# Third block of a three-block network: copies, logarithms, banks and the first C·B products placed elsewhere between the normalisation and the state-space stage

## The reference, cut to what matters

```
x = first_block(...)                                   # ends with rms_norm(h, final_norm_g)
h = _rmsnorm(x, norm_w) * (1 + scale) + shift          # "C" in the kernel; x's own norm is "D"
proj = einsum("bsd,de->bse", h, w_in)                  # 1024 x 1024 by 1024 x IN_COLS
z_ssm, xbc, dt_raw, q, k, v, z_att, f_logit, g_logit = split(proj)
xbc = silu(causal_depthwise_conv(xbc, conv_w, conv_b)) # 4 taps; 1280 channels = 10 blocks of 128
xs, B, C = split(xbc, [1024, 1152])                    # B, C: 2 groups x 64 states
dt = softplus(dt_raw + dt_bias); a = -dt * exp(a_log)  # the step sizes
cb = einsum("bclgn,bcsgn->bgcls", C, B)                # per chunk of 128 tokens: "C.B"
y = (cb * L) @ (xs * dt) + (terms of earlier chunks) + d_skip * xs
```

## Time and profile before

| | us |
|---|---|
| median of 3 runs (lowest, highest) | 2923.1 (2921.4, 2924.74) |
| the profiled execution | 2922.75 |
| its span | 2921.4 |
| PE busy | 2786.5, 95% |
| DVE busy | 1591.5, 54% |
| ACT busy | 1356.0, 46% |
| POOL busy | 851.7, 29% |

### The profile page before, as it was taken

The page is one execution under the profiler, slowest core; times in us unless marked ns, Lnnn a source line. Parts: engine busy times, 40 slices in busy tenths (PEclk is TensorE's granted clock), DMA queues, the critical chain, the costliest instruction groups (busy, mean ns, idle before and its releaser), DMA issues.

```text
span 2921.4 us, 36300 instructions
## 1 busy us (share of the span) xinstructions
PE 2786.5 (95%) x13800; PEld 2278.1 (78%) x13800; DVE 1591.5 (54%) x2766; ACT 1356.0 (46%) x2486; POOL 851.7 (29%) x668
## 2 busy tenths in 40 slices
PE   8999999999999999998997999999999999999997
PEld 6778777777788888887774877778787888887875
DVE  6667774644388888887467765531002444433034
ACT  5657864334367666674435334541113333333122
POOL 0334441223345445542121222133221111112331
PEclk9999999999999999999998999999999999999998
DMA  3101131211100000003110200133111000101231
GB/s 130 40 29 41 40 130 64 94 66 37 33 10 10 10 10 10 17 23 139 49 58 27 101 29 23 30 98 90 58 51 37 30 30 30 30 30 44 72 116 72
DMA packets 54443, 148.77 MB, mean 51 GB/s; under 512 B 6144, under 2 KB 14976, under 8 KB 54272
## 3 DMA queue, kind: packets, MB, share of 16 engines
q1 hardware_dynamic: 54272, 146.46, 15.3%
HBM read 129.66 MB, written 16.78 MB: 50 GB/s over the span
## 4 chain that ended last, share of the span: by engine, by line
PE 85%; DVE 6%; ACT 5%; issue 3%; POOL 1%; DMA 0%; ACTq 0%; DVEq 0%; POOLq 0%
PE ps L327 79%; PE ps L445 4%; ACT t L311 1%; PE ps L2611 1%; PE ps L768 1%; DVE t L1665 0%; ACT t L807 0%; DVE t L898 0%; DVE t L2957 0%; DVE t L867 0%; POOL t L318 0%; DVE t L1295 0%; DVE t L1678 0%; ACT L394 0%; POOL t L2862 0%
## 5 line engine op out<-in xcount | busy, mean ns | idle before, releaser
L327 PE MATMUL ps<-t,t 128*128 128x512 f32 (+5 forms) x11912 | 2622.8, 379 | 107.8 <-ACT t L2056 9.5
L327 PEld LDWEIGHTS ps<-t,t 128*128 128x128 f32 (+2 forms) x11912 | 2075.9, 185 | 583.3 <-issue 113.9
L318 POOL TENSOR_TENSOR t<-t,t 128x1024 fp32r<-128x1024 f32 (+2 forms) x169 | 359.9, 2130 | 1267.6 <-ACT t L311 1267.0
L311 ACT ACTIVATE t<-t 128x1024 fp32r<-128x1024 f32 (+2 forms) x205 | 187.0, 913 | 678.6 <-PE ps L327 678.6
L1721 POOL TENSOR_SCALAR t<-t,t 128x1024 f32<-128x1024 f32 x128 | 145.2, 1134 | 183.0 <-DVE t L1671 180.0
L1665 DVE TENSOR_TENSOR t<-ps,t 128x512 fp32r<-128x512 f32 x256 | 164.2, 682 | 15.8 <-ACT t L1582 13.9
L445 PE MATMUL ps<-t,t 128*128 128x128 f32 x1176 | 160.5, 274 | 12.7 <-DVE t L1665 7.6
L445 PEld LDWEIGHTS ps<-t,t 128*128 128x128 f32 x1176 | 131.9, 141 | 36.5 <-issue 24.7
L1678 DVE TENSOR_REDUCE t<-ps 128x1 f32<-128x1024 f32 x128 | 154.1, 1204 | 2.2 <-PE ps L327 2.2
L1582 ACT ACTIVATE t<-ps 128x512 fp32r<-128x512 f32 x256 | 140.2, 592 | 11.3 <-PE ps L445 7.2
L1590 ACT ACTIVATE t<-ps,t 128x1024 f32<-128x1024 f32 x128 | 142.8, 1116 | 1.9 <-DVE t L1678 1.5
(11 more groups left out here) (219 smaller groups left out, 2429.6 us busy)
## 6 DMA issues: line engine op xcount, KB each, us to landing
t<-in_wflat SPq DMA_DIRECT2D x156, 512.0 KB, 3.6
t<-in_wada SPq DMA_DIRECT2D x48, 256.0 KB, 3.9
t<-in_xT SPq DMA_DIRECT2D x16, 512.0 KB, 7.0
t<-in_wflat SPq DMA_DIRECT2D x32, 128.0 KB, 2.0
hd<-t SPq DMA_DIRECT2D x8, 512.0 KB, 3.0
t<-hd SPq DMA_DIRECT2D x8, 512.0 KB, 7.5
x2d<-t SPq DMA_DIRECT2D x8, 512.0 KB, 6.8
md<-t SPq DMA_DIRECT2D x16, 256.0 KB, 4.4
```

Of the source, the lines that this page charges most:

```text
L311: ac.activation(parts(i)[0][:, 0:n], raw[i % 2][:, 0:n], ACT.Copy).then_inc(*on.up(ac, "whi", i))
L318: e.tensor_tensor(lo[:, 0:n], raw[i % 2][:, 0:n], hi[:, 0:n], ALU.subtract) \
L327: return pe.matmul(o, l, r, start=start, stop=stop)
```

## The change

Four edits in these stages:

1. The first two copies out of PSUM (`conv_in` of blocks 0 and 1, half 0) stand in ACT's program after the fourth high part of the second half, where they stood after `rstd`.
2. The two logarithms of `rstd` "D" stand together, and then the two exponentials. `w_hi` of `DTF` and of block 2 follow at once.
3. The two halves of `DTF` go to banks 4 and 5 (last used by the totals of norm "C"), and don't take a turn of `next_bank`; every later bank of the stage moves.
4. `products(0)` stands on PE between the two halves of block 7, the last of the convolution, in two banks that `next_bank` gives; `products_out(0)` stands on DVE before the taps of block 7's second half.

```
-            def scalar():
+            def scalar(first_inputs):
...
                 for k in range(8):
                     high_part(k, 1)
+                    if k == 3:
+                        first_inputs()
+                for hf in range(2):
+                    on.wait_ge(ac, "sums/tot", "D", hf)
+                    ac.activation(RB[:, half(hf)], ps[:, bank["D", hf], :], ACT.Ln, bias=eps[:, 0:1], scale=1.0 / T).then_inc(*on.up(ac, "ln", "D", hf))
+                for hf in range(2):
+                    on.wait_ge(ac, "ln", "D", hf)
+                    ac.activation(RB[:, half(hf)], RB[:, half(hf)], ACT.Exp, scale=-0.5).then_inc(*on.up(ac, "rstd", "D", hf))
...
-                            bank[DTF, x] = lin(DTF, x, next_bank(*every), Uh, Ul, need_c, [("dt", x)])
+                            bank[DTF, x] = lin(DTF, x, 4 + x, Uh, Ul, need_c, [("dt", x)])
...
+                    if (n, hf) == (7, 1):
+                        products(0, (next_bank(*every), next_bank(*every)))
                     bank[XB[q], hf] = lin(XB[q], hf, next_bank(*every), Uh, Ul, need_c, [("conv in", q, hf)])
...
                     if (n, hf) == (4, 0):
                         sums()
+                    if (n, hf) == (7, 1):
+                        products_out(0)
...
-                norm_scalar()
-                for hf in range(2):
-                    rstd("D", hf, bank["D", hf], RB, T)
+                def first_inputs():
+                    for x in range(2):
+                        conv_in(*todo[x])
+
+                norm_scalar(first_inputs)
+                w_hi(XB[0] + 2)
+                w_hi(XB[1] + 2)
...
-                    if x == 1:
-                        w_hi(XB[0] + 2)
-                        w_hi(XB[1] + 2)
+                    if x > 1:
+                        conv_in(q, n, hf)
                     if x:
                         smooth(*todo[x - 1])
...
-                products(0)
                 for g in range(2):
                     segments(8 * g)
...
-                            products(1)
+                            products(1, (4, 5))
...
             def vector():
                 everything_in(dv)
-                products_out(0)
```

More of the change, by code:

```diff
@@ L1896, in program, with products, products_out @@
         tv = tot[:, :].rearrange("p (c h) -> p c h", c=8)
+        def products(g, banks):
+            rg = slice(64 * g, 64 * g + 64)
+            for c2, b in enumerate(banks):
+                bank["cb", g, c2] = b
+                wait_bank(b)
+                on.wait_ge(pe, "xb", 9, 1)
+                for c in range(4):
+                    cc = slice((4 * c2 + c) * P, (4 * c2 + c + 1) * P)
+                    t = mm(ps[:, b, c * P:(c + 1) * P], BT[rg, cc], CT[rg, cc], True, True)
+                t.then_inc(*on.up(pe, "cb", g, c2))
+                freed[b] = [("cb out", g, c2)]
+        def products_out(g):
+            for c2 in range(2):
+                on.wait_ge(dv, "cb", g, c2)
+                src = ps[:, bank["cb", g, c2], :].rearrange("p (c n) -> p c n", c=4)
+                dv.tensor_tensor(CB[:, 4 * c2:4 * c2 + 4, :], src, tri.unsqueeze(1).to_broadcast([P, 4, P]), ALU.mult) \
+                    .then_inc(*on.up(dv, "cb out", g, c2))
         def stage_conv():
@@ L2051, in scalar @@
                         w_hi(XB[q] + 2)
-                    on.wait_ge(ac, "mm", XB[q], hf)
-                    earlier = [p for p in range(q) if X_ORDER[p] % 2 == n % 2]
-                    if earlier:
-                        on.wait_ge(ac, "conv", earlier[-1], 1, 3)
-                    ac.activation(xin[n % 2][:, 3 + hf * H:3 + hf * H + H], ps[:, bank[XB[q], hf], :], ACT.Copy).then_inc(*on.up(ac, "conv in", q, hf))
-                    if x == 1:
-                        w_hi(XB[0] + 2)
-                        w_hi(XB[1] + 2)
+                    if x > 1:
+                        conv_in(q, n, hf)
                     if x:
@@ L2062, in scalar, with conv_in @@
                 smooth(*todo[-1])
+            def conv_in(q, n, hf):
+                on.wait_ge(ac, "mm", XB[q], hf)
+                earlier = [p for p in range(q) if X_ORDER[p] % 2 == n % 2]
+                if earlier:
+                    on.wait_ge(ac, "conv", earlier[-1], 1, 3)
+                ac.activation(xin[n % 2][:, 3 + hf * H:3 + hf * H + H], ps[:, bank[XB[q], hf], :], ACT.Copy).then_inc(*on.up(ac, "conv in", q, hf))
             def smooth(q, n, hf):
@@ L2169, in tensor @@
                         if t == 2:
-                            products(1)
+                            products(1, (4, 5))
                 on.ends(pe, "end ssd", "pe")
-            def products(g):
-                rg = slice(64 * g, 64 * g + 64)
-                for c2 in range(2):
-                    b = 4 + c2
-                    wait_bank(b)
-                    on.wait_ge(pe, "xb", 9, 1)
-                    for c in range(4):
-                        cc = slice((4 * c2 + c) * P, (4 * c2 + c + 1) * P)
-                        t = mm(ps[:, b, c * P:(c + 1) * P], BT[rg, cc], CT[rg, cc], True, True)
-                    t.then_inc(*on.up(pe, "cb", g, c2))
-                    freed[b] = [("cb out", g, c2)]
             def gate_pe(t, hf):
@@ L2284, in vector @@
                 on.ends(dv, "end ssd", "dv")
-            def products_out(g):
-                for c2 in range(2):
-                    on.wait_ge(dv, "cb", g, c2)
-                    src = ps[:, 4 + c2, :].rearrange("p (c n) -> p c n", c=4)
-                    dv.tensor_tensor(CB[:, 4 * c2:4 * c2 + 4, :], src, tri.unsqueeze(1).to_broadcast([P, 4, P]), ALU.mult) \
-                        .then_inc(*on.up(dv, "cb out", g, c2))
             def pair_pick(t):
```

## The result

| | before | changed |
|---|---|---|
| median (lowest, highest), us | 2922.74 (2921.4, 2924.74), 4 runs | 2905.82 (2903.6, 2908.13), 4 runs |
| profiled execution, us | 2922.75 | 2905.76 |
| its span, us | 2921.4 | 2904.4 |

The ratio is 0.9941, interval 0.9928 to 0.9954. The direction was right and the size wrong: the larger part of what is missing in the forecast lies behind the edited stages.

The account below looks back on a forecast made before the run. PE was taken to bound the kernel, ending the chain for 85% of the span. Gains 8.2 + 1.55 + 1.6 = 11.35 from 2922.75 gave 2911.4, forecast 2911.5 us, range 2908.3 to 2916.3.

Parts of the forecast that it names:

- Copies amid the high parts: ACT's first two copies after the fourth high part: cost 0, at most 0.5 us; DVE's first taps start at 1580.4.
- Joined logarithms: ACT before DTF: two table loads fewer, about 5.0 us instead of 7.77, so high weights start at 1584.7.
- rival 2: Joining the logarithms saves nothing, ACT's block ends at 1587.3, PE resumes at 1588.8 on a slow clock: 2915.6 us; chance 0.03.
- Gap at `DTF`: PE's 9.51 us wait before DTF shrinks to 1.3 us, awaiting POOL's low weights: gain 8.2 us, between 7.0 and 8.6.
- The clock stays up: Behind the gap at DTF PE's clock stays at 1.00: gain 1.55 us, bounds 0 and 1.55.
- Fed to the end of the convolution: PE doesn't wait again before the convolution ends; block 3's low weights come 1.1 us early: cost 0, at most 2 us.
- rival 1: PE's wait moves to block 3, or DTF's gap is 2 us or more and the clock falls: 2914 to 2915; chance 0.12.
- End stage: After the convolution's last matmul (E), gate's block starts at E + 12.0, not E + 16.02: gain 1.6 us, between -0.5 and 2.5.
- Rival 3: Only one of the two gaps closes: 2913.9 if the end stage doesn't gain, 2921 if the first gap stays; chance 0.09.
- Local sum: The edited stages' terms, 8.2 + 1.55 + 1.6, together a gain of 11.35 us.
- From 1715.99 on ... what is gained is kept: From the gate's block on, order and banks are as before and PE runs 20.46 us without a gap, so gains stay.
- five rivals: Numbered alternatives: moved wait, joining saves nothing, one gap closes, copies too early (2923 and above, 0.03), banks kept by another reader.

Follow-up runs that it names:

- shift4: Changed kernel with 4 extra matmuls of 512 columns, read by nothing, on PE before block 5 of the convolution; median 2909.24 us.
- shift56: Changed kernel with 56 extra matmuls of 512 columns, read by nothing, on PE before block 5 of the convolution; median 2921.85 us.
- no_copies: Changed kernel with the first two copies put back behind logarithms and exponentials; median 2911.04 us.
- early_chunks: Changed kernel with B's transposes, five x chunks, their scalings and first decays moved ahead of and amid block 7's last half; median 2913.54 us.
- ec2_plus19: Changed kernel with early B transposes, five x chunks and scalings, DVE's pick ahead of the taps, plus 19 extra matmuls before block 5; median 2906.01 us.
- before_plus7: Kernel before with 7 extra matmuls of 512 columns on PE ahead of the second gate block; median 2922.89 us.
- no_products: Changed kernel with the C·B products and their masking back in the state-space stage, in banks 4 and 5; median 2911.30 us.
- shift8: Changed kernel with 8 extra matmuls of 512 columns, read by nothing, on PE before block 5 of the convolution; median 2909.81 us.
- no_logs: Changed kernel with load, logarithm, load, exponential run twice again; median 2913.52 us.
- no_banks2: Changed kernel with DTF's halves back in next_bank's banks and the products in banks 4 and 5, other banks unmoved; median 2913.20 us.

## Why the prediction was wrong, step by step

- *Copies amid the high parts: cost 0, DVE's taps from 1580.4.* Right: the copies ran at 1573.71 (forecast 1574.3), taps started at 1580.02, and PE reached `DTF` after 38.06 us, as against 38.21.
- *Joined logarithms: about 5.0 us, high weights at 1584.7.* Right in size: two loads, 4.94 us from 1579.12 to 1584.06. The start is 0.64 early, more than the 0.3 that I had allowed; 0.35 of this is the head. The rule that I had weighed, of the Trainium skill, page "ScalarE: Activation LUTs", section "Table sets: the hidden batching unit", by which logarithm and exponential share one table set, isn't what this trace does: going from logarithm to exponential took a load of 1.28 us each time, and rival 2 with it falls.
- *Gap at `DTF` 1.3 us, gain 8.2.* Measured 1.16 and 8.35. POOL began 0.42 us behind ACT and took 0.94, until 1585.42, and PE resumed at 1585.52. The forecast had the row name POOL's low weights as the releaser; it names ACT's L311. But the high weights of `DTF` were there by 1584.48, when POOL began to work from them, so the wait that ended last was POOL's, as forecast.
- *The clock stays up: 1.55.* Right: 1.00 behind the gap. From `DTF` to the convolution's end PE took 106.38 us (to 1691.90), before 105.60 (to 1699.97); with the products' 2.05 in it, the clock gave 1.27, 0.28 less than the term.
- *Fed to the end of the convolution, 1.1 us to spare at block 3.* Right, and for the reason given: POOL's low part was held off for 8.54 us, until 1606.56, 2.26 us after `residual` ended (1593.61 + 10.69), before 2.25. By the forecast's count PE came to need it at 1585.52 + 22.2 = 1607.7, so 1.1 us was to spare. Nothing on PE waited (rival 1).
- *End stage: gate's block at E + 12.0, and 0.4 more for a slow clock.* The gate's 82 matmuls and the wait behind them take 21.03 us before (1715.99 to 1737.02); counted back from 1724.59 they began at 1703.56, E + 11.66, and no 0.4 was lost, as the clock had risen by 1702.7. That is 0.74 more gain than forecast. ACT's copy of B released PE at E + 7.76, forecast 7.7. It was PE's slow transposes that came last: 16 of them in 3.17 us, and the clock, 0.53 over them, rose at their end. This agrees with the earlier trace rows and not with the rule of the Trainium skill, page "TensorE: Matmul & The Clock Gate", section "Part 4: PE-mode transpose", by which the full clock doesn't engage for transposes, though a rise 0.2 us before other matmuls shows less than the one at 1713.56 did. Rival 3 had this stage worth -0.8; it was worth more than forecast.
- *Local sum.* 8.35 - 0.78 + 4.36 + 0.15 = 12.08, forecast 11.35. Alone, with the 0.35 of the head, this would have given 2922.75 - 12.08 - 0.35 = 2910.3, inside the range. (2911.4 + 0.35 is 2911.75 and not 2911.5, a slip in the forecast that changes nothing.)
- ***From 1715.99 on ... what is gained is kept.*** This step failed. Order and banks were as I said, and PE's gaps are as long as before; but what PE does behind them isn't paid at the same clock in the two kernels, and work added upstream of the same program was enough to move a tail by 1.2 to 3.2 us (shift4 to shift56). I took the slow stretches of the tail for a constant, gave them neither a term nor a bound, and looked at no gap of the tail. Measured: 4.58 us less, 4.39 of it in PE's busy time. Why the clock answers equal gaps differently stays open. None of the five rivals occurred.

The range should have had this term on both sides. Over the kernels above whose later banks are unchanged, tails lie between 1163.5 and 1168.2 us: a spread of 4.7 us. That the kernel before sat at the slow end of it and the changed one at the fast end couldn't be known without runs; no run shows a way to forecast it.

## What to carry to other kernels

PE has gaps of 2 to 5 us in unchanged stages here, and changes upstream came with another granted clock behind them, worth up to 4.7 us, as much as a good edit. Put that into the range of a forecast, and judge a small edit by the stretch that it touches, cut out between two gaps that both traces have, rather than by the total; even that stretch held 0.7 us of chance in one trace (no_copies). Where several waits end close together, taking back a single one can lose nearly half of what all four gained locally (5.7 and 5.6 of 12.1 us): price them together. And move everything that the last wait has behind it: early_chunks left one short instruction of DVE behind the taps, and PE stood 7 us before it.

## What the runs showed of the hardware

- Added work isn't paid at its own time. Between the gap at 1546 and the last gap, 4.4 us of added matmuls cost 1.1 us (ec2_plus19), 1.6 us cost nothing (before_plus7), and 0.92 us cost 3.5 (shift4).
- Gaps of equal length and releaser, 3.54 us, left the clock at 0.62 over the next 7.1 us in the kernel before and at 1.00 in the changed one; at 0.63 in no_products and at 1.00 in shift8, at the same place within 0.04 us.
- A gap of 1.16 us left the clock at 1.00 (changed kernel), 2.17 us gave 0.63 over the next 3.5 (no_copies), and 3.66 and 3.73 us gave 0.50 over the next 3.5 (no_logs, no_banks2). With the 3.54 us above this is no rule of length alone.
- DVE's 16 back-to-back instructions held a POOL instruction for 8.54 us that takes 2.39 by itself, and let it go 2.26 us after their own end, as before the change (2.25, after 6.12 us). In no_copies POOL's same instruction began at 1606.92, 2.45 us behind the first of the sixteen, and took 2.53 us, while the sixteen took 12.83 us instead of 10.69. What decides which of the two waits, no run here shows.
